# Order of the high and low products in the feature-major chunks of a two-layer block

## What is computed

```python
# first layer, cut
proj = h @ w_in[l]                      # q, k, v and the branches' inputs
x = x + (g_a * y_a + g_b * y_b + g_c * y_c) @ w_out[l]
x = x + jnp.square(jax.nn.relu(h @ w_mlp_up[l])) @ w_mlp_down[l]
# second layer, cut
h = rmsnorm(x, g_mix) @ w_in
x = x + jnp.concatenate([y_ssd, y_att], axis=-1) @ w_out
u = rmsnorm(x, g_mlp) @ w_up
return x + jnp.square(jax.nn.relu(u)) @ w_down
```

## Time and profile before

| | |
|---|---|
| three runs, median (lowest to highest) | 2652.4 us (2650.54 to 2652.66) |
| the profiled execution | 2650.98 us |
| its span, first to last instruction | 2649.3 us |
| TensorE busy, of the span | 100% |
| DVE, ACT, POOL busy | 75%, 52%, 1% |
| mean DMA rate | 193 GB/s |

### The profile page before, as it was taken

One profiled execution on the slowest core, in us unless ns is written; L12 is line 12 of the kernel. 1 busy time (PEld: TensorE's weight loads), 2 busy tenths in 40 slices (PEclk: granted clock), 3 DMA queues, 4 the chain that ended last, 5 costly groups with the idle time before them and its releaser, 6 DMA issues.

```text
span 2649.3 us, 39598 instructions
## 1 busy us (share of the span) xinstructions
PE 2640.2 (100%) x13478; PEld 2233.5 (84%) x13478; DVE 1986.9 (75%) x2876; ACT 1366.9 (52%) x1865; POOL 30.3 (1%) x64
## 2 busy tenths in 40 slices
PE   9999999999999999999999999999999999999999
PEld 7888888888888888888888888888788888888887
DVE  6687876555555778798797567878787978879886
ACT  6455555444444554555554454456555555455453
POOL 0100000000000000000000000000000000000000
PEclk9999999999999999999999999999999999999999
DMA  7655556665655566556566555545555655655565
GB/s 277 236 175 182 190 173 197 204 201 194 203 191 188 177 199 205 187 196 198 190 206 210 190 176 175 173 150 191 171 175 190 199 198 192 205 190 196 187 205 175
DMA packets 141721, 511.06 MB, mean 193 GB/s; under 512 B 16134, under 2 KB 16439, under 8 KB 141464
## 3 DMA queue, kind: packets, MB, share of 16 engines
q1 hardware_dynamic: 136312, 493.86, 55.9%
q0 software_dynamic: 3840, 12.86, 1.5%
q10 hardware_dynamic: 1440, 2.62, 0.3%
HBM read 505.08 MB, written 4.21 MB: 192 GB/s over the span
## 4 chain that ended last, share of the span: by engine, by line
PE 96%; DVE 2%; ACT 1%; DMA 0%; issue 0%; SPq 0%; ACTq 0%; DVEq 0%
PE acc L1955 26%; PE acc L1952 13%; PE acc L1973 5%; PE acc L1991 4%; PE acc L1993 4%; PE acc L1992 4%; PE pS L1991 3%; PE pS L1993 3%; PE pT L1993 3%; PE pT L1991 3%; PE pS L1992 3%; PE pT L1992 3%; PE acc L1970 2%; PE pO L1991 2%; PE pO L1993 2%; PE pG L1993 2%
## 5 line engine op out<-in xcount | busy, mean ns | idle before, releaser
L1104 DVE TENSOR_TENSOR wlo<-raw,whi 128x1024 fp32r<-128x1024 f32 x938 | 1143.4, 1223 | 446.4 <-ACT whi L614 440.5
L614 ACT ACTIVATE whi<-raw 128x1024 fp32r<-128x1024 f32 x938 | 990.0, 1057 | 793.7 <-PE pT L1993 243.1
L1955 PE MATMUL acc<-a_w,whi 128*128 128x512 f32 x2944 | 935.8, 397 | 0.1
L1952 PEld LDWEIGHTS acc<-a_w,wlo 128*128 128x128 f32 x2944 | 553.2, 188 | 129.4
L1952 PE MATMUL acc<-a_w,wlo 128*128 128x256 f32 x2944 | 578.6, 278 | 0.0
L1955 PEld LDWEIGHTS acc<-a_w,whi 128*128 128x128 f32 x2944 | 451.5, 189 | 2.5 <-DVE a_w L1157 0.8
L1973 PE MATMUL acc<-a_w,whi 128*128 128x512 f32 x592 | 198.4, 404 | 0.0
L825 ACT ACTIVATE t<-acc 128x256 f32<-128x256 f32 x128 | 48.9, 382 | 170.0 <-PE acc L1955 169.9
L1970 PEld LDWEIGHTS acc<-a_w,wlo 128*128 128x128 f32 x592 | 111.4, 188 | 24.5
L1970 PE MATMUL acc<-a_w,wlo 128*128 128x256 f32 x592 | 116.8, 279 | 0.0
L1500 DVE TENSOR_TENSOR t<-acc,t 128x256 f32<-128x256 f32 x128 | 54.0, 422 | 74.9 <-ACT t L825 74.8
(11 more groups left out here) (496 smaller groups left out, 3962.8 us busy)
## 6 DMA issues: line engine op xcount, KB each, us to landing
raw<-stream SPq DMA_DIRECT2D x938, 512.0 KB, 3.4
gbias<-gateb POOLq DMA_DIRECT2D x12, 256.0 KB, 4.1
X<-x_rows POOLq DMA_DIRECT2D x4, 512.0 KB, 6.8
bias_scratch<-brow POOLq DMA_DIRECT2D x8, 256.0 KB, 5.5
q<-bias_scratch POOLq DMA_DIRECT2D x8, 256.0 KB, 3.8
out<-X ACTq DMA_DIRECT2D x8, 256.0 KB, 5.3
xF<-x SPq DMA_DIRECT2D x6, 256.0 KB, 6.8
bias<-bias_scratch POOLq DMA_DIRECT2D x8, 128.0 KB, 4.1
```

The source lines that it names most:

```text
L614: A(whi[:, slot, :], raw[:, slot, :], ACT.Copy).then_inc(s.hi_done, 1)
L1104: TT(wlo[:, slot, :], raw[:, slot, :], whi[:, slot, :].bitcast(F32), SUB).then_inc(s.lo_done, 1)
L1952: low = lambda: MM(ps[:, 0:T], wl, wide[:, k0 + k, 0:T], start=False, stop=False, skip_group_check=True)
L1955: last = MM(ps, wh, wide[:, k0 + k, :], start=start and k == 0, stop=not start and k == KC - 1, skip_group_check=True)
```

## The change

The products of a feature-major chunk are issued in another order: first the eight highs, then the eight lows. The lows add to the first half of the bank for even k and to the second half for odd k; the halves are added in the end, as before. The waits for late activation tiles stay ahead of every second high. `WARM` is 8 in place of 5.

```diff
--- before.py
+++ after.py
@@ -72,7 +72,7 @@
 A_MLP2 = A_L2 + L2_EVACS
 
 
-WARM = 5
+WARM = 8
 COLS = 512
 NG = D // COLS
 G_Y = 2
@@ -1948,13 +1948,10 @@
                 for k in range(KC):
                     if late is not None and k % 2 == 0:
                         pe.wait_ge(s.a_ready, late + k0 + k + 2)
-                    wh, wl = (w[:, slot, P * k:P * k + P] for w in (whi, wlo))
-                    low = lambda: MM(ps[:, 0:T], wl, wide[:, k0 + k, 0:T], start=False, stop=False, skip_group_check=True)
-                    if k % 2:
-                        low()
-                    last = MM(ps, wh, wide[:, k0 + k, :], start=start and k == 0, stop=not start and k == KC - 1, skip_group_check=True)
-                    if k % 2 == 0:
-                        low()
+                    MM(ps, whi[:, slot, P * k:P * k + P], wide[:, k0 + k, :], start=start and k == 0, stop=False, skip_group_check=True)
+                for k in range(KC):
+                    last = MM(ps[:, T * (k % 2):T * (k % 2) + T], wlo[:, slot, P * k:P * k + P], wide[:, k0 + k, 0:T], start=False,
+                              stop=not start and k == KC - 1, skip_group_check=True)
                 last.then_inc(s.mm_done, 1)
 
             def half_unit(c, u, half):
@@ -1965,14 +1962,11 @@
                 slot = c.mod(NSLOT)
                 pe.wait_ge(s.lo_done, c.value(1))
                 for k in range(KC):
-                    wh, wl = (w[:, slot, P * k:P * k + P] for w in (whi, wlo))
-                    m = 8 * half + k
-                    low = lambda: MM(ps[:, 0:T], wl, a_w[:, m, 0:T], start=False, stop=False, skip_group_check=True)
-                    if k % 2:
-                        low()
-                    last = MM(ps, wh, a_w[:, m, :], start=half == 0 and k == 0, stop=half == 1 and k == KC - 1, skip_group_check=True)
-                    if k % 2 == 0:
-                        low()
+                    MM(ps, whi[:, slot, P * k:P * k + P], a_w[:, 8 * half + k, :], start=half == 0 and k == 0, stop=False,
+                       skip_group_check=True)
+                for k in range(KC):
+                    last = MM(ps[:, T * (k % 2):T * (k % 2) + T], wlo[:, slot, P * k:P * k + P], a_w[:, 8 * half + k, 0:T], start=False,
+                              stop=half == 1 and k == KC - 1, skip_group_check=True)
                 last.then_inc(s.mm_done, 1)
 
             def chunk_tok(c, i, banks, src, k0, first, last, units=None, corner=False):
```

## The result

The new kernel takes 2654.64 us (median of 22 executions, 2654.2 to 2655.25); the kernel before, timed in turn with it, 2650.76 us (22 executions, 2650.28 to 2652.66). The ratio is 1.0014 with a 95% interval of 1.0008 to 1.0019: 3.9 us slower (2.1 to 5.0), where 4.5 us faster was forecast. That is inside the range given and under the 0.2% that the prediction called no change. The three runs of before that it started from had a median 1.6 us above the longer measurement; what makes single executions that much longer stands under warm8.

A forecast was written before the change was run, and what follows sets the result against it. TensorE's rate of starting products was taken as the bound. Reordered chunks -5.9 us, late inputs +1.4, halves and zero products 0, sum -4.5: 2652.4 - 4.5 = 2648 us, range 2622 to 2661.

The forecast's parts named there:

- What bounds the kernel: Whole kernel: TensorE is always busy at full clock, so only how fast it starts successive products counts.
- The lows in a row: Eight 256-column lows in each reordered chunk: 0.120 us each, a fixed 0.0133 us over the stream.
- 0.1133: Rival on the lows: each costs half a high, 2.720 us a chunk, -28 us, 2624 us; chance 0.32.
- load-bound 0.125: Rival on the lows: weight loads need 0.125 us, 2.813 a chunk, +13 us, 2666 us; slower lows or warm-up 0.18.
- The highs in a row: Eight 512-column highs in each reordered chunk: 0.2267 us each, 1.813 us together, at most 0.01 for the step from lows.
- The two halves of the bank: Lows adding to the bank's halves in turn: no stall from adding to the same place, priced at nothing.
- The late inputs: Second chunk of each feed-forward's first unit: more products behind the last wait, 0.71 us later, two layers, +1.4 us.
- Eight zero products: Program start: extra passes hidden under the wait for the first low weights, 0 us; +2.2 us if all at low clock.
- Nothing changes: Rival: a low costs 0.1217 us in any order, leaving only +1.4 us, 2654 us; an edge of the first case.

The follow-up runs named there:

- warm8: The kernel before with eight zero products in place of five: 2650.63 against 2650.70 us, ratio 0.9999.
- run1: The kernel before with highs and lows strictly alternating, except in chunks with late inputs: 2665.38 against 2650.70 us, ratio 1.0056.
- run4: The kernel before with four highs, four lows, twice a chunk, except in chunks with late inputs: 2657.63 against 2650.59 us, ratio 1.0026.
- mix6262: The kernel before with six highs, six lows, two highs, two lows a chunk, except with late inputs: 2649.59 against 2650.55 us, ratio 0.9996.
- run16: The kernel before with highs first and lows first in alternate chunks, so runs of 16, except with late inputs: 2649.70 against 2650.59 us, ratio 0.9996.
- mix14: The kernel before; chunks alternate 8 highs, 8 lows with 6 lows, 2 highs, 2 lows, 6 highs, except with late inputs: 2646.98 against 2650.63 us, 0.9987.
- run8alt: The new kernel's order and turn of halves, but late-input chunks and five zero products as before: 2653.16 against 2650.59 us, ratio 1.0009.
- all256: The new order with each high split into two 256-column products with the same weight tile: 2690.06 against the kernel before's 2650.70 us, ratio 1.0148.
- pairs_alt: The kernel before, with the lows of odd k adding to the second half of the bank: 2650.72 against 2650.59 us, ratio 1.0000.
- late_new: The kernel before with the new order and turn of halves only in the four late-input chunks: 2652.01 against 2650.70 us, ratio 1.0005.

## Why the prediction was wrong

All sums beside each other, against 2.7733 us:

| order | steps low to high a chunk | chunk, us | toll a step, ns |
|---|---|---|---|
| run1 | 8 | 2.8263 | 6.6 (0 in one stretch) |
| before, pairs | 4 | 2.7866 | 3.3 |
| run4 | 2 | 2.8059 | 16.3 |
| after, eights | 1 | 2.7925 | 19.2 |
| mix6262 | 1, with HH LL in it | 2.7797 | 6.4 |
| run16 | 1/2 | 2.7834 | 20 |
| mix14 | 1/2, with HH LL in it | 2.7766 | 6.6 |

The chunk times are those of long stretches, and the totals moved by less where the order departs far from pairs: by 438 chunks run4 would be 8.5 us above before and mix14 4.4 below, and 7.0 and 3.7 were measured. Only six groups of 32 chunks are as long as the window; the rest stand in shorter stretches or alone.

- *What bounds the kernel.* Right: TensorE is busy throughout before and after, and the 2.6 us of run8alt are its chunks' 5.9 ns times 438.
- *The lows in a row.* Right: 0.120 us, shown by eight in a row, by fourteen, and by all256. Both rivals on them fell with it: not 0.1133, and no load-bound 0.125. The Trainium skill (TensorE: Matmul & The Clock Gate, "Back-to-back issue gap") gives N/2.4 GHz plus 2.5 ns for the gap of a single product at the full clock, which for 256 columns is an estimated 109 ns; the runs don't agree, with 120.
- *The highs in a row.* **This step failed**: "at most 0.01 us goes to the step from lows to highs. Eight highs: 1.813 us." They took 1.840, less 0.007 on the lows behind: 0.019 us net. The row it was read from the earlier trace rows stood behind two lows, and after a pair the step costs little. The 13.3 ns that the forecast took off a chunk were the toll of four pairs, and no term of the sum put another toll in their place. The chunk has one step now in place of four, but the one costs 19.2 ns and the four of before cost 13.3. The sum by this term: (2.7733 + 0.0192 - 2.7866) x 442 = +2.6 us, in place of -5.9.
- *The two halves of the bank.* Right: nothing (pairs_alt).
- *The late inputs.* Right: +1.4 forecast, +1.3 in late_new (its interval holds zero), and the next chunk starts 0.71 us later behind DVE's last tile.
- *Eight zero products.* Right for the median: nothing (warm8), and at most 0.09 us in the new kernel's trace. That they may spare some executions a drop of the clock was not foreseen.

The sign depended on 0.013 us a chunk, and the value assumed for the step was taken from another run length. The rival "Nothing changes" comes to 2654 us, next to the measured time, but by luck: it has lows of 0.1217, which no run shows, and counts from 2652.4. The sentence "I am wrong if ... highs reading this operand in a row need more than 0.2267" named the place.

Open: what in TensorE makes the toll, and why strict alternation has two paces. The runs show that it depends on the length of the runs, that it comes with the step from 256 to 512 columns, and that the half of the bank, the weight's tile, the head of a chunk, the late inputs and the start have no part in it. No run had products of other widths than these, or other activations.

## What to carry to other kernels

When products of two lengths alternate, price a sequence by the time between starts in that very sequence: a spacing measured behind two short products did not hold behind eight. If long runs can't be avoided, a pair of the long and a pair of the short kind ahead of the long run took most of the loss away in long stretches here (6.6 ns in place of 20); in short ones mix6262 gave part of it back. And when activation tiles come late, every product moved behind the last wait is paid in full, however cheap it is elsewhere.

## What was not expected of the hardware

- After eight or more products of 256 columns, the next five of 512 start 0.228 to 0.236 us apart in place of 0.2267 (after, run16, and all256 on other tiles), 28 ns too much, of which the next two short ones give 8 back. After four short ones the net is 16 ns, after two 3.3.
- The same order of products ran at 0.347 us a pair in one stretch and at 0.353 in the other feed-forward groups of 32 chunks (run1).
- A fixed 0.0133 us on each fp32r product over its columns at 2.4 GHz, alike for 256 and 512 columns, also where the weight tile is the one used before and is loaded again (all256).
- With five zero products at the start, 17 of 110 executions of the kernel before were some 1.7 us longer, with eight none of 33; the one trace of such an execution (pairs_alt) has the clock at 1.2 GHz from 9.37 to 12.78 us, behind the wait for the first low weights.
